# The first block's start in a new order: constants behind the first weights, gates' rows inside the convolutions, z around the norms

## The reference, cut to what matters

```python
proj = h @ w_in      # gq gk gv gz ga gb | fq fk fv ff | gate_a gate_b
# branch A: gated DeltaNet, 4 heads of 128
qkv = silu(causal_depthwise_conv(concat(gq, gk, gv), conv_w))      # 12 column blocks of 128
q, k = l2norm(q) * 128 ** -0.5, l2norm(k)
g, beta = -exp(a_log) * softplus(ga + dt_bias), sigmoid(gb)
o = gated_delta_rule(q, k, v, g, beta)
y_a = (rmsnorm(o) * norm_w * silu(gz)) @ w_out_gdn
# branch B: forgetting attention, 8 heads of 64
y_b = attention(fq, fk, fv, cumsum(log_sigmoid(ff + f_bias))) @ w_out_fox
h = layernorm(alpha * h + (sigmoid(gate_a) * y_a + sigmoid(gate_b) * y_b) @ w_o)
# PEER: 8 heads, 128 x 128 product keys, the 16 best experts of each head
scores -> top 16 of each half -> top 16 of the pairs -> expert ids, softmax gates
h = layernorm(alpha * h + sum_k gelu(h . u[expert_k]) * gate_k * v[expert_k])
```

## Time and profile before

| | us |
|---|---|
| median of 3 runs (3955.14 to 3964.44) | 3963.78 |
| the profiled execution | 3961.94 |
| its span, first to last instruction | 3959.9 |
| PE busy | 2528.5 |
| DVE busy | 2252.0 |
| POOL busy | 2282.8 |
| ACT busy | 532.3 |

### The profile page before, as it was taken

How to read it: one execution, slowest core, us unless ns; L and a number is a source line. 1 busy time by engine, 2 the same in 40 slices (tenths; PEclk the granted TensorE clock), 3 DMA queues, 4 the chain that set the end, 5 groups by cost and what they waited for, 6 DMA issues and landing times.

```text
span 3959.9 us, 36514 instructions
## 1 busy us (share of the span) xinstructions
PE 2528.5 (64%) x11992; PEld 1554.1 (39%) x11992; DVE 2252.0 (57%) x5313; ACT 532.3 (13%) x1223; POOL 2282.8 (58%) x2086
## 2 busy tenths in 40 slices
PE   6888874456987876656977866567787710123354
PEld 5676763343644543433735534333554300000010
DVE  4143699765357776655368776555356678644300
ACT  2121320211002201121003102111101000000000
POOL 1000255467555666677556666667665577777765
PEclk8889887776988887776989988767898855555567
DMA  4313688589998899899999999999999999999998
GB/s 139 107 59 144 228 318 311 165 289 358 402 392 346 332 400 365 311 373 359 416 397 355 369 408 331 326 332 358 379 410 377 351 336 351 370 358 363 360 368 317
DMA packets 367618, 1290.17 MB, mean 326 GB/s; under 512 B 39468, under 2 KB 68148, under 8 KB 362308
## 3 DMA queue, kind: packets, MB, share of 16 engines
q0 software_dynamic: 294912, 1073.87, 71.7%
q1 hardware_dynamic: 66760, 201.39, 13.9%
q10 hardware_dynamic: 5760, 12.59, 0.8%
HBM read 1274.72 MB, written 12.98 MB: 325 GB/s over the span
## 4 chain that ended last, share of the span: by engine, by line
PE 26%; POOL 22%; issue 18%; DVE 17%; DMA 7%; another core or an unknown queue 4%; DVEq 3%; ACT 2%; SPq 0%; ACTq 0%; POOLq 0%
PE banks L1314 11%; POOL ring L647 11%; POOL ring L635 11%; DVE ring L991 8%; DMA ring<-in_ev,idxT 6%; PE banks L1303 5%; PE banks L1324 4%; PE banks L1576 1%; PE banks L1364 1%; PE banks L1319 1%; DVE arena L944 1%; DVE arena L946 1%; DMA wslot<-in_w_mix 1%; DVEq L941 1%
## 5 line engine op out<-in xcount | busy, mean ns | idle before, releaser
L635 POOL DMA_INDIRECT ring<-in_eu,eidx x1024 | 1170.3, 1143 | 1158.5 <-DVE eidx L1270 421.9
L647 POOL DMA_INDIRECT ring<-in_ev,idxT x1024 | 1100.8, 1075 | 496.6 <-issue 296.0
L991 DVE CUSTOM_DVE_ANT_0 ring<-ring,h_cur 128x1024 f32<-128x1024 f32 x1024 | 1216.1, 1221 | 293.9 <-DMA ring<-in_eu,eidx 251.8
L1303 PE MATMUL banks<-ring,wide 128*32 128x512 f32 x4096 | 721.3, 826 | 613.2 <-DMA ring<-in_ev,idxT 523.1
L1314 PE MATMUL banks<-arena,wslot 128*128 128x256 f32 (+1 forms) x3248 | 769.3, 394 | 76.0 <-issue 32.2
L1314 PEld LDWEIGHTS banks<-arena,wslot 128*128 128x128 f32 (+1 forms) x3248 | 630.3, 197 | 246.4 <-issue 142.8
L1303 PEld LDWEIGHTS banks<-ring,wide 128*32 128x32 f32 x4096 | 147.3, 135 | 1031.9 <-issue 1003.8
L1324 PE MATMUL banks<-arena 128*128 128x128 f32 x1408 | 235.4, 331 | 70.1 <-ACT arena L794 28.2
L1324 PEld LDWEIGHTS banks<-arena 128*128 128x128 f32 x1408 | 215.8, 239 | 104.3 <-issue 43.4
L1314 PE MATMUL banks<-ring,wslot 128*128 128x256 f32 (+1 forms) x656 | 155.0, 394 | 20.4 <-POOL wide L621 14.6
L1319 PE MATMUL banks<-ident,arena 128*128 128x128 f32 x216 | 50.8, 392 | 181.4 <-DVE arena L963 47.2
(11 more groups left out here) (230 smaller groups left out, 2385.1 us busy)
## 6 DMA issues: line engine op xcount, KB each, us to landing
wslot<-in_w_pq SPq DMA_DIRECT2D x64, 576.0 KB
wslot<-in_w_mix SPq DMA_DIRECT2D x24, 1536.0 KB
wslot<-in_w_qkv SPq DMA_DIRECT2D x48, 512.0 KB
wslot<-in_w_fqk SPq DMA_DIRECT2D x32, 512.0 KB
wslot<-in_w_out SPq DMA_DIRECT2D x8, 2048.0 KB
ring<-in_eu,eidx POOLq DMA_INDIRECT x1024
ring<-in_ev,idxT POOLq DMA_INDIRECT x1024
wslot<-in_w_z SPq DMA_DIRECT2D x16, 512.0 KB
```

The costliest lines, as they stand in the source:

```text
L635: pool.indirect_dma_start(out=ring[:, UPOS[k] % NR, :], out_offset=None, in_=eu, in_offset=bass.IndirectOffsetOnAxis(ap=eidx[:, n % (2 * T ...
L647: pool.indirect_dma_start(out=ring[:, VPOS[k] % NR, :], out_offset=None, in_=ev, in_offset=bass.IndirectOffsetOnAxis(ap=idxT[:, n % (2 * T ...
L991: dve.tensor_tensor_reduce(out=row, in0=row, in1=h_cur[:, n % 3, :], scale=1.0, scalar=0.0, op0=ALU.mult, op1=ALU.add, accum_out=dots[:, n ...
L1303: last = pe.matmul(BY[k][32 * j:32 * j + 32, :], wide32[:, at:at + 32], ring[:, VPOS[4 * q + j] % NR, k * 512:(k + 1) * 512], start=(m == ...
```

## The change

Four things change in the order of work, and no arithmetic does.

1. The constants. SP issues `xT`, the weights of `sm` and of `conv 0` first, then the four small loads, then the other weights. The two broadcasts `ln2B` go to `prod 0` of block 0, under a semaphore of their own. POOL signals once behind the memsets of `fcarry` and `halo` (its first two), and a second time where it did before; PE waits for the second only in `rT`, ACT and DVE in the new unit `nrm`.
2. The gates' rows. `sm` is now the projection alone, on PE. The chain on DVE and ACT is a unit of its own, `sv`. In block 0 it stands between `conv 5` and `conv 6`; in later blocks right behind `sm`. The store of the rows moves from `conv 3` to `conv 9` in block 0, and `acc` and `raw` of block 0 move to `ring`, since the chain's buffers overlap theirs.
3. The norms are a unit of their own, `nrm`, ahead of `prod 0` in every block.
4. In block 0 the units behind the convolutions are now `rT`, `z 0`, `nrm`, `z 1`, `prod 0`. Before they were `rT`, `prod 0` with the norms, `z 0`, `z 1`. What follows closes up: fqk 0 and 1 stand behind `prod 0` and not behind `lev 0`, and so on to the first attention step, which stands behind `lev 4` and not behind `lev 5`.

SHARE has entries for the new units. With the eight added list entries the plan of `pace()` moves slightly in blocks 1 to 3.

```diff
-PROJECT = ([("sm", 0)] + [("conv", c) for c in range(13)] + [("z", 0), ("z", 1), ("rT", 0)]
+PROJECT = ([("sm", 0), ("sv", 0)] + [("conv", c) for c in range(13)] + [("z", 0), ("z", 1), ("rT", 0)]
 DELTA = [u for c in range(TT) for u in
-         [("prod", c)] + [v for l in range(LEVELS) ...
+         ([] if c else [("nrm", 0)]) + [("prod", c)] + [v for l in range(LEVELS) ...
...
-    early = [("sm", 0)] + [("conv", c) for c in range(13)] + [("rT", 0)]
+    early = ([("sm", 0)] + [("conv", c) for c in range(6)] + [("sv", 0)] + [("conv", c) for c in range(6, 13)] + [("rT", 0)]
+             + [("z", 0), ("nrm", 0), ("z", 1)])
...
-    for n, (kind, i) in enumerate(DELTA):
+    for n, (kind, i) in enumerate(DELTA[1:]):
         units.append((kind, 0, i))
-        upto = (n + 1) * len(beside) // len(DELTA)
+        upto = (n + 1) * len(beside) // (len(DELTA) - 1)
...
-SHARE = {"sm": 8.0, ... "prod": 18.0, ...
+SHARE = {"sm": 1.0, "sv": 7.0, "nrm": 6.0, ... "prod": 12.0, ...
...
+        acc = ring[:, 13, 0:2 * T].rearrange("p (a b) -> p a b", a=2)
+        raw = [ring[:, 14, 0:2 * (T + 3)].rearrange("p (a b) -> p a b", a=2)] + [raw_] * (NB - 1)
...
         @block.sync
-            for dst, src in ((cw[:, :, :], conv_w), (bias_c[:, :], bias96), (alog_c[:, :], alog96),
-                             (normB[:, :], norm_w.to_broadcast([P, P]))):
-                sp.dma_start(dst, src).then_inc(s_cst, 16)
-            for k in range(2):
-                sp.dma_start(ln2B[:, k, :], ln[2 + k:3 + k, :].to_broadcast([P, D])).then_inc(s_cst, 16)
...
-                if c == 3:
+                if c == (3 if b else 9):
                     sp.wait_ge(s_rows, b + 1)
...
             def prod(b, c):
+                if c == 0 and b == 0:
+                    for k in range(2):
+                        sp.dma_start(ln2B[:, k, :], ln[2 + k:3 + k, :].to_broadcast([P, D])).then_inc(s_ln2, 16)
...
             fetch_xT(0)
-            for item in range(4):
+            for item in range(2):
+                fetch(*PITEMS[item])
+            for dst, src in ((cw[:, :, :], conv_w), (bias_c[:, :], bias96), (alog_c[:, :], alog96),
+                             (normB[:, :], norm_w.to_broadcast([P, P]))):
+                sp.dma_start(dst, src).then_inc(s_cst, 16)
+            for item in range(2, 4):
                 fetch(*PITEMS[item])
...
         @block.gpsimd
+            pool.memset(fcarry[:, :], 0.0)
+            pool.memset(halo[:, :, :], 0.0).then_inc(s_const, 1)
...
         @block.scalar
-            act.wait_ge(s_const, 1)
-            act.wait_ge(s_cst, 16 * 6)
+            act.wait_ge(s_cst, 16 * 4)
...
             def conv(b, c):
-                if c == 0:
-                    act.wait_ge(s_rows, b + 1)
                 if b:
+                    if c == 0:
+                        act.wait_ge(s_rows, b + 1)
...
+            def nrm(b, i):
+                if b == 0:
+                    act.wait_ge(s_const, 2)
+                for k in range(4):
+                    act.wait_ge(g["ssum"], 4 * b + k + 1)
+                    act.activation(flat(nr[:, 2 * k:2 * k + 2, :]), B[k][:, :], ACT.Ln, bias=eps_l2[:, :])
+                act.drain()
+                act.activation(nr, nr, ACT.Exp, scale=-0.5).then_inc(g["norm"], 1)
...
         @block.vector
-            def sm_(b, i):
+            def sv(b, i):
...
+            def nrm(b, i):
+                if b == 0:
+                    dve.wait_ge(s_const, 2)
+                dve.wait_ge(s_ixT, b)
+                dve.wait_ge(s_rTe, b + 1)
+                dve.wait_ge(s_rowst, 16 * (b + 1))
+                for j in range(2):
+                    dve.wait_ge(s_silu[j], 6 * (b + 1))
+                dve.drain()
+                dve.tensor_tensor(sq, qkvS[:, 0:8, :], qkvS[:, 0:8, :], ALU.mult).then_inc(g["sq"], 1)
...
         @block.tensor
-            pe.wait_ge(s_const, 1)
...
             def rT(b, i):
+                if b == 0:
+                    pe.wait_ge(s_const, 2)
                 pe.wait_ge(s_rows, b + 1)
```

More of the change, by code:

```diff
@@ L82 @@
 UNITS = order()
[L83 removed]
+SHARE = {"sm": 1.0, "sv": 7.0, "nrm": 6.0, "conv": 3.5, "z": 5.0, "rT": 1.5, "fqk": 3.5, "fv": 5.0, "prod": 12.0, "lev": 5.0, "wu": 4.0,
          "ws": 3.0, "o": 4.0, "og": 8.0, "att": 2.5, "ato": 1.5, "ot": 4.0, "mix": 9.0, "wo": 6.0, "ln": 9.0,
@@ L1621, in idx @@
                 last.then_inc(s_iT, 1)
-            work = {"sm": sm_, "conv": conv, "z": z, "rT": rT, "fqk": fqk, "fv": fv, "prod": prod, "lev": lev, "wu": wu,
+            work = {"sm": sm_, "conv": conv, "z": z, "rT": rT, "fqk": fqk, "fv": fv, "nrm": nrm, "prod": prod, "lev": lev, "wu": wu,
                     "ws": ws, "o": o_, "og": og_, "att": att, "ato": ato, "ot": ot, "gt": gt, "mix": mix, "wo": wo, "ln": ln_, "top": top,
```

76 lines of the change are left out of this document (30 added, 46 removed).

## The result

The changed kernel took 3910.65 us (median of 4, 3903.35 to 3916.44), the kernel before beside it 3964.11 (median of 4): a ratio of 0.9865 [0.9843, 0.9887], or 53.5 us less. The profiled execution took 3916.44 us (span 3914.4) against 3961.94: 45.5 us less. It is the slowest of the four changed ones; the pair of traces shows 8 us less than the medians.

The account below looks back on a forecast made before the run. Block 0 was taken as a chain of engines, with DMA gathers filling the rest behind it. Terms 9.8 + 1.8 + 16.3 + 0 + 4 = 32 us off 3961.9 gave 3931 us, range 3912 to 3948 for 8 in 10.

Parts of the forecast that it names:

- Step 1, the start: Block 0's first loads: xT and sm's weights issued first let PE start near 8.0 us, not 14.55; 6.5 us gained.
- Step 2, the rows: Gates' rows and convolutions in block 0: last SiLU starts at 62.9, 9.8 us earlier, 6.5 of them from the start.
- The clock: PE in block 0's conv 10 and 11: full speed assumed behind a wait of 4.0 us; 3 us longer otherwise.
- the bound of 3: Block 0's conv 10 and 11: two convolutions at half clock end at 61.9, not 58.7, delaying z 0 by 3.2 us.
- Step 3, the norms: Norms of block 0: z 0 covers the wait and keeps PE's clock up for the sums; 1.8 us, bounds 0 and 2.
- Step 4, z: Block 0 from z to the first level: products begin at 90.2, with fqk 0 and 1 done; 16.3 us gained.
- The rival that the levels and the attention steps take z's place: Block 0's second half: levels, ACT's scalings and attention bind, half of z's gain returns as waits; 3944 us, chance 0.10.
- Step 5, the late level: Block 0's lev 5 moves to the attention steps, bound by ACT and DVE as much as PE: 1 us lost, 0 to 6.
- The better clock for the first level: Block 0's first level products, half of whose 6 us ran at the lower clock: 1 us gained, 0 to 2.
- Step 6, later blocks: Blocks 1 to 3: nrm lets DVE do two dot products before prod 0; 4 us, 0 to 7; plan 0, 10 either way.
- Gathered rows ahead of the norms: Rival, blocks 2 and 3: waits for v rows between sums and prod 0 cost time; 3944 to 3977 us, chance 0.05.
- The start moved: Answers the rival that xT arrives no sooner and PE starts at 12 to 13: 5 us lost, 3936, chance 0.06.

Follow-up runs that it names:

- block 0 alone: Kernel before with block 0's new order only, blocks 1 to 3 with the old list and costs: 0.9932 on chip B, 0.9933 on chip E.
- the second experiment: Changed kernel with block 0's attention steps one unit later, behind both lev 4 and lev 5: 3764.82 us, 0.9877 against the kernel before on chip D.

## Why the prediction was right or wrong

**Step 1, the start: right.** Forecast 8.0, measured 7.04. What it brings at the first choice, 10 to 11 us, was not in the sum.

**Step 2, the rows: the size right, the reason in part wrong.** The last SiLU starts at 62.57 (forecast 62.9) behind a wait of 4.37 us (4.0). The gain belongs to the removed wait of ACT; the place in the middle costs 3.3 us. I never summed the other order.

**The clock: wrong.** I took full speed behind the wait of `conv 10`, and argued from a stretch that ended at 85.00, inside PE's wait, that a wait of 4 us leaves the clock alone. The rows just behind it, in the same trace of the kernel before, say the opposite:

```profile
81.30:85.00 3.70, 0.00 (x0) 0.00 (x0) 0.76 (x5) 3.61 (x3) 0.00 (x0) 1.00 0.00 0
85.00:88.40 3.40, 0.66 (x4) 0.42 (x4) 3.02 (x4) 2.79 (x6) 0.00 (x0) 0.65 0.00 0
88.40:90.40 2.00, 1.92 (x9) 1.92 (x10) 1.93 (x5) 0.00 (x0) 0.00 (x0) 0.50 0.00 0
```

So the stretch after a wait has to be read too. It is not always the one after: ahead of the first attention step of the same trace PE stood still from 176.45 to 180.46, and the clock read 1.00 to 178, 0.59 to 179 and 0.50 to 180. In `conv 10` and `11` the low clock cost 1.9 us (8.78 for two convolutions in place of 6.9), which stood within the bound of 3. That bound was called two convolutions at half clock, but it is one; two would take 13.8 us and end at 65.6, not 61.9.

The rule of the Trainium skill that I had set against the row ("TensorE: Matmul & The Clock Gate", section "Why this matters for your kernels", on idle gaps between bursts of matmuls) holds in each of these places: behind 4.37 us, behind the wait from 81.29 on in the kernel before, and behind the 3.21 us ahead of the first attention step. Near 3 us the traces of this case go both ways: behind the wait of 2.85 us ahead of the transposes at 294.49 the changed kernel had 1.00 on A, C and E and 0.60 on D.

**Step 3, the norms: wrong, and small.** Forecast 1.8 us, measured 0.15 (15.69 less 15.54). The sums are faster by 1.6 us, but 0.9 are lost since z 0 ends 1.12 us behind the squares, and so did not come for nothing: part of the clock's 1.9 us of step 2 is passed on here. Another 0.5 is lost to ACT, whose table load and four Ln take 3.7 us in a row from the first sum on (67.97 to 71.69). DVE's last multiplication ends at 78.11 and not 76.8.

**Step 4, z: right up to attention.** The first level's products start 19.7 us earlier (forecast 20.8), at 91.32 (90.2), with two projections done. The 1.1 us are what step 3 lacked. The rival that the levels and the attention steps take z's place is answered: with the attention steps behind `lev 5` in both kernels, z's place and the norms with it are worth 24 us at the first choice, more than the 18.1 of steps 3 and 4.

**Step 5, the late level: mis-sized, and the largest error of block 0.** I put 1 us for `lev 5` behind the first attention step, within 0 to 6, and the runs show 15: with both levels ahead of the steps the first update comes 8.7 us and the second's end 15.0 earlier. The sum had looked at whether ACT and DVE could take a level more, and not at what PE has left to do while v is under way, nor at its clock behind it. Both kernels of the pair on chip D differ there: a wait of 3.15 us against 0.23, and a clock of 0.50 against 1.00. How the 8.7 become 15.0 in the second chunk was not traced. Against the kernel before, less shows (from 26.1 to 24.2 and 21.0), and that kernel too had the wait and the low clock. The better clock for the first level, 1 us in the sum, did not come either: from its first products to the next level's 13.5 us passed (91.32 to 104.85) against 13.0 (111.01 to 123.97).

**Block 0: 28 forecast, 24.0 at its first choice on A** (24.7 on D, 411.9 for 436.6), passed on in full, and measured alone as 26 and 25.5. The number came out right by luck: the start and z's place gave 11 us more than forecast, and the attention steps' place took 15.

**Step 6, later blocks: the step that failed.** Forecast 4 us (0 to 7 for the norms' wait, and 10 either way for the plan, which I put at 0). Alone they measured 10.7 and 5.7. The wait for the norms fell in blocks 1 to 3 of A from 26.0 us (29.2 less 3.2 in block 0) to 17.1 (6.2, 6.4 and 4.5), that is by 8.9, where I had 7.2 and counted 4. That is a term mis-sized by a few us. But A's pair shows some 20 in these blocks, and no step holds them. Their dates beside those of chip D, changed less before:

| | A | D |
|---|---|---|
| first choice, block 0 | -24.0 | -24.7 |
| eighth choice, block 0 | -27.0 | -25.2 |
| first choice, block 1 | -35.0 | -32.2 |
| first choice, block 2 | -34.9 | -29.1 |
| first choice, block 3 | -35.9 | -22.2 |
| last choice | -47.1 | -21.3 |
| span | -45.5 | -27.9 |

Block 1 gives 7 to 8 us on both: there the norms' wait and the plan act beside DMA engines that are not full (0.79). On D it is given back behind the gathers, as the prediction had it. On A it is kept, and 11 more come between the first and the last choice of block 3. These are single traces: the changed kernel begins block 3's choice at 2893.1 on C and 2899.2 on E against 2903.1 on D, so the D column moves by up to 10 us with the trace that is taken. On E, beside block 0 alone on the same chip (2915.0 there), the later blocks' part is 15.8 us at that date and 21.4 in the span (3780.1 less 3758.7). So a chip as fast as D can keep it too. **What stays open** is why. The gathers of A are slower (367 GB/s from 1000 to 3300 us; before on D 382), so the same plan meets other waits; that this is the cause was not shown, since no other chip was as slow. Nor is one pair of traces much: 35 executions of the kernel before on chip B lie between 3782 and 3825 us. On C, D and E the forecast of 32 us stands among 27, 40 and 37, by the same luck as in block 0.

**The other rivals.** Gathered rows ahead of the norms did not become a bound: PE's waits for v rows from 400 us on are, beside the 523.1 in 121 of the earlier trace rows,

```profile
PE banks L1312 <- DMA ring<-in_ev,idxT: 539.9, 112, 23.3
```

17 us more in fewer, and the end came sooner nonetheless. The start moved, and the DMA engines lost nothing of it.

## What to carry to other kernels

When a unit is moved, ask at each end of the move what PE does while a transfer or another engine is under way: work of its own in that gap is worth twice, the wait and the clock behind it. Here two levels ahead of the first attention step kept 15 us of block 0 in the trace, though the medians do not show them beyond their intervals. When an experiment takes a unit out of its place, look at what else moves in the list: undoing z's place alone also moved the attention steps, and without the second experiment its trace would have told the wrong story. And ask of each wait which instruction needs it: ACT's wait for the rows stood ahead of copies that did not, and taking it away was worth more than the new place of the rows. A table of one chip's date by date differences beside another's tells what belongs to the change; block 0's 24 us were the same on A, B, D and E (23.4 to 24.7), the rest was not.

## What the runs showed of the hardware

- The same kernel takes 3964 us on one chip and 3802 to 3808 on four others. Block 0, without gathers, is the same to 1 us (first choice at 435.9 on A, 436.6 on D); the stretches with gathers are not (last choice at 3190.1 and 3079.8).
- PE's clock stood at 1.00 through an idle stretch of 3.7 us (81.3 to 85.0) and read 0.65 and 0.50 in the stretches behind it. In another wait of the same trace (176.45 to 180.46) it read 0.59 and 0.50 while PE still stood idle.
- Behind the same wait of 2.85 us the changed kernel had a clock of 1.00 in three traces (A, C, E) and 0.60 in one (D).
- A table load of ACT took 1.28 us, and the next activation began 0.02 us behind it (67.97 and 69.27).
